# A mixture-of-experts block on one core: the router stage's work in a new order on all engines

## The chip, the cores and the metric

One core of a Trainium2 chip. The metric is the device time of one execution in microseconds (us). "Before" is the median of three runs of the kernel as it was.

## The reference

One layer of a decoder trunk over 1024 tokens of width 1024, all in float32. The parts that matter here come after the three mixers have left their outputs side by side in one row of 1024 per token (`ymix`):

```python
y   = ymix @ w_out                              # output projection
x2  = x + gate * rmsnorm(y) * g_post            # residual
h   = rmsnorm(x2) * (1 + scale) + shift         # input of the MoE
scores = sigmoid(h @ w_router)                  # 64 experts
biased = scores + e_bias
# 8 groups of 8 experts; the 4 groups with the best sum of their top 2
# then the 8 best experts of those groups
top_w = scores[top] / sum(scores[top]) * 2.5
shared = (silu(h @ ws1) * (h @ ws3)) @ ws2      # shared expert, width 256
# each expert e: its tokens through silu(xb @ w1[e]) * (xb @ w3[e]) @ w2[e]
```

## The kernel before, in words

The kernel runs in stages that follow each other: input projection and modulation, attention, the RWKV recurrence, the router stage (`norm_route`, L1530 to L2087), the 64 experts (`experts`, L2090) and the last norm. A stage is a block: every engine has its own written-out list of instructions, each in order, and semaphores join them. A new block starts when all engines have ended the old one.

The router stage works on 8 tiles (NT) of 128 tokens. Two lanes of buffers take turns: tile t uses lane t % 2. A lane has four banks of PSUM: t0 and t1 for transposes, for the router's product (t1) and the list positions (t0), p0 and p1 for the output projection, the shared expert's hidden layer (p1), its transposes (p0) and its result (p0, p1). Per tile the pieces are these, by the names that the code and the change use:

- TensorE (PE): `transpose_y` (L1957, 8 transposes), `project` (L1968, 48 matmuls: two halves n of 512 columns, 8 steps k, three passes of float32r parts), `up` (L1997, the shared expert's first layer, two halves of 12 matmuls), `transpose_h` (L2011, 8), `place` (L2020 and L2021, two small products that count the tokens before each one), `route` (L2027, the router's product in plain float32: 8 steps, 16 records of 64 columns), `transpose_act` (L2034, 2), `down` (L2042, 4 products in float32, 8 records of 512 columns).
- ScalarE (ACT): `y_norm` (L1688 to L1692: the squares of both halves, then the root), `y_cast` (L1682, L1683: high part of the next but one transposed tile), `x_norm` (L1697 to L1699), `h_copy` (L1706, L1707: transposed h out of PSUM, which `route` and `place` wait for), `h_cast` (L1711), `shared_sig` (L1716 to L1718), `score_exp` (L1723), `shared_out` (L1733), and once per kernel the four casts of the shared weights (L1756).
- VectorE (DVE): `x_rows` (L1780 to L1790: sum of squares, two scalings out of p0 and p1, and the addition of x), `y_rest` (L1770, L1771: low part of the transposed tile), `h_scaled` (L1798), `h_rows` (L1802), `shared_arg` (L1807), `shared_act` (L1814, L1815), `copy_act` (L1822), `logits` (L1827), `select` (L1832 to L1861, 26 small steps one after the other), `h_rest` (L1775), `places` (L1868 to L1872), and after the last tile `block_counts`, `block_ends`, `block_rows` (L1876 to L1896) and `first_rows` (L1900 to L1902).
- GpSimd (POOL): for each tile, after `places`, one store of the weights (L1657) and eight indirect scatters of token numbers into the experts' lists (L1659); after the last tile a gather of the list rows (L1663), which waits for all scatters, and four gathers of the first blocks' tokens (L1670).
- SyncE (SP): loads and stores, among them those of the shared result (L1642) and the loads of the first two experts' weights (L2365, L2372), in an order of its own, which waits for the same semaphores.

The order is written out in a loop over r from -1 to 9. In turn r, PE does `project(r+1)`, `transpose_y(r+2)`, `up(r-2)`, `transpose_h(r)`, `place(r-1)`, `route(r)`, `transpose_act(r-2)`, `down(r-2)`. DVE does `x_rows(r+1)`, `y_rest(r+2)`, `h_scaled(r+1)`, `shared_arg(r-2)`, `h_rows(r+1)`, `places(r-1)`, `shared_act(r-2)`, `logits(r)`, `copy_act(r-2)`, `select(r)`, `h_rest(r)`. The few waits that matter: `route(r)` waits for `h_copy(r)`; `transpose_act` for `shared_act`; `down` for `copy_act`; `transpose_h(r)` for `y_rest(r+2)`, since both use t0 and t1 of a lane; `project(t)` for `shared_out(t-4)`; `up(t)` for the scalings of tile t+2.

## Time and profile before

| | us |
|---|---|
| median of 3 runs | 1972.87 |
| lowest and highest run | 1970.88, 1981.24 |
| the profiled execution, its own time | 1981.13 |
| its span, first to last instruction | 1979.3 |
| router stage in it | 689.3 to 961.7 |
| PE busy over the span | 1770.1 (89%) |
| DVE, ACT, POOL busy | 1411.6, 1133.6, 454.5 |

The times of the trace are microseconds from the span's start. A matmul's end is modelled, so that the records of matmuls in a row overlap: what one costs is the distance between two starts. PEclk is the share of full speed that TensorE's clock was granted, 1.00 for 2.4 GHz and 0.50 for 1.2 GHz.

### The profile page before, as it was taken

How to read it: one execution, taken by the hardware profiler on the slowest of the kernel's cores; microseconds unless marked ns; L12 is line 12 of the kernel's file. 1: busy time of each engine (PE TensorE's matmuls, PEld its weight loads, DVE VectorE, ACT ScalarE, POOL GpSimd, SP SyncE). 2: the span in 40 equal slices, each digit the busy share in tenths (PEclk: the TensorE clock that was granted, in tenths of full speed). 3: DMA queues.
4: the chain of work that ended last, by engine and by line, in shares of the span. 5: the costliest groups of instructions: out<-in, count | busy, mean ns of one | idle time of the engine just before them, and what ended most of it. 6: DMA issues, size and time to landing. Idle time of an engine off the chain costs nothing. (4 is left out here: it accounts for less than half of the span.)

```text
span 1979.3 us, 38771 instructions
## 1 busy us (share of the span) xinstructions
PE 1770.1 (89%) x10357; PEld 1361.8 (69%) x10358; DVE 1411.6 (71%) x2637; ACT 1133.6 (57%) x2184; POOL 454.5 (23%) x361
## 2 busy tenths in 40 slices
PE   3899999777699788998599999999999999999992
PEld 3787887454488666765377777777777677777771
DVE  6587740687488566445388888888888788888885
ACT  3411220576466443322377777777777677777774
POOL 0011000000122103135122332333233333333331
PEclk9999999898799888988799999999999999999996
DMA  9267610300200163314779979799989989899965
GB/s 348 81 193 214 183 49 27 128 18 16 89 6 11 50 236 95 81 53 109 243 236 303 292 217 301 222 314 319 279 259 295 311 283 288 249 315 309 297 180 181
DMA packets 168094, 380.06 MB, mean 192 GB/s; under 512 B 31189, under 2 KB 43822, under 8 KB 164924
## 3 DMA queue, kind: packets, MB, share of 16 engines
q1 hardware_dynamic: 132844, 288.38, 41.9%
q0 software_dynamic: 35168, 90.60, 18.9%
q8 instruction: 50, 0.82, 0.2%
q14 instruction: 32, 0.26, 0.1%
HBM read 333.82 MB, written 82.13 MB: 210 GB/s over the span
## 5 line engine op out<-in xcount | busy, mean ns | idle before, releaser
L2267 DVE TENSOR_TENSOR w_low<-w_experts,w_high 128x1024 fp32r<-128x1024 f32 x392 | 462.0, 1220 | 103.6 <-issue 68.0
L2216 ACT CAST w_high<-w_experts 128x1024 fp32r x394 | 394.0, 1050 | 97.0 <-issue 77.2
L2198 POOL DMA_INDIRECT acc<-y_rows,scatter_idx x96 | 185.4, 1931 | 612.7 <-DMA acc<-y_rows,scatter_idx 354.2
L2329 PE MATMUL ps_h<-w_high,xT_high 128*128 128x512 f32 x776 | 315.9, 407 | 10.7 <-DVE xT_low L2282 10.5
L2329 PE MATMUL ps_h<-w_high,xT_low 128*128 128x512 f32 x776 | 307.7, 397 | 0.0
L2329 PE MATMUL ps_h<-w_low,xT_high 128*128 128x512 f32 x776 | 307.5, 396 | 0.0
L2351 PE MATMUL ps_y<-w_experts,actT 128*128 x384 | 182.1, 597 | 2.3 <-DVE actT_low L2273 2.3
L2329 PEld LDWEIGHTS ps_h<-w_high,xT_high 128*128 128x128 f32 x776 | 147.3, 190 | 43.4 <-issue 6.7
L2329 PEld LDWEIGHTS ps_h<-w_high,xT_low 128*128 128x128 f32 x776 | 146.2, 188 | 35.4
L2329 PEld LDWEIGHTS ps_h<-w_low,xT_high 128*128 128x128 f32 x776 | 146.6, 189 | 31.0
L2182 POOL DMA_INDIRECT gathered<-h,idx x96 | 130.5, 1359 | 58.1 <-DVE idx L2260 29.1
L2224 ACT CAST w_high<-w_experts 128x512 fp32r x192 | 110.2, 625 | 27.3 <-issue 24.4
L2276 DVE TENSOR_TENSOR w_low<-w_experts,w_high 128x512 fp32r<-128x512 f32 x192 | 123.2, 682 | 0.2
L2321 PEld LDWEIGHTS ps_x<-ident,gathered 128*128 128x128 f32 x784 | 103.9, 193 | 16.7 <-issue 7.7
L2355 PE MATMUL ps_y<-w_high,actT_high 128*128 128x512 f32 x192 | 114.5, 596 | 0.0
L2321 PE MATMUL ps_x<-ident,gathered 128*128 128x128 f32 x784 | 104.8, 277 | 6.9 <-PEq L1532 6.9
L506 PE MATMUL pbank<-w_in_high,hT_high 128*128 128x512 f32 x256 | 103.4, 404 | 6.8 <-DVE w_in_low L339 6.8
L506 PE MATMUL pbank<-w_in_low,hT_high 128*128 128x512 f32 x256 | 101.7, 397 | 0.0
L506 PE MATMUL pbank<-w_in_high,hT_low 128*128 128x512 f32 x256 | 101.4, 396 | 0.0
L2351 PEld LDWEIGHTS ps_y<-w_experts,actT 128*128 128x128 f32 x384 | 66.1, 192 | 48.7 <-issue 48.7
L884 POOL TENSOR_TENSOR r_k<-p_mixed,k 128x256 f32<-128x256 f32 x8 | 6.0, 748 | 341.1 <-DVE operands L1142 341.1
L2209 ACT CAST xT_high<-ps_x 128x512 fp32r<-128x512 f32 x98 | 57.4, 585 | 41.5 <-PE ps_x L2321 40.6
(440 smaller groups left out, 3627.6 us busy)
## 6 DMA issues: line engine op xcount, KB each, us to landing
w_experts<-in_exp_w SPq DMA_DIRECT2D x512, 256.0 KB
w_experts<-in_exp_w SPq DMA_DIRECT2D x128, 512.0 KB
qT<-in_w_ada POOLq DMA_DIRECT2D x16, 1024.0 KB, 7.8
w_raw<-in_w_in SPq DMA_DIRECT2D x24, 512.0 KB, 7.9
w_ada<-in_w_ada SPq DMA_DIRECT2D x8, 1024.0 KB, 12.0
p_mixed<-mixed SPq DMA_DIRECT2D x8, 512.0 KB, 8.3
w_out<-in_w_out SPq DMA_DIRECT2D x1, 4096.0 KB, 12.6
x_kept<-x SPq DMA_DIRECT2D x8, 512.0 KB
```

Source lines behind the costliest of these rows:

```text
L506: q = mm(bank[u % RING][:], lhs, rhs, start=(k == 0 and i == 0), stop=(k == KC - 1 and i == 2))
L2182: pool.indirect_dma_start(xg[j][:], None, dr["h2"], bass.IndirectOffsetOnAxis(ap=idx[j][:], axis=0), bounds_check=S - 1, oob_is_err=False) ...
L2198: pool.indirect_dma_start(dr["acc"], bass.IndirectOffsetOnAxis(ap=sidx[j][:], axis=0), y[j % 2][:], None, bounds_check=S - 1, oob_is_err=F ...
L2209: act.copy(xT[0][:, 0:4, :], ps_x[0][:].rearrange("p (k n) -> p k n", k=4))
L2216: act.copy(w13_s[par][0][:, which, k], w13[:, bass.ds(w, 1), which, k].squeeze(1)).then_inc(w_high, 1)
L2224: act.copy(w2_s[half][0], w2[:, bass.ds(w, 1), 1, half * BANK:(half + 1) * BANK].squeeze(1)).then_inc(d_high, 1)
L2267: dve.tensor_tensor(w13_s[par][1][:, which, k], w13[:, bass.ds(w, 1), which, k].squeeze(1), w13_s[par][0][:, which, k], ALU.subtract).then ...
L2276: dve.tensor_tensor(w2_s[half][1], w2[:, bass.ds(w, 1), 1, half * BANK:(half + 1) * BANK].squeeze(1), w2_s[half][0], ALU.subtract).then_in ...
L2321: q = pe.transpose(ps_x[k // 4][:, (k % 4) * P:(k % 4 + 1) * P], xg[j][:, 0:D].rearrange("p (c k) -> p k c", k=KC)[:, k, :], ident[:])
L2329: q = pe.matmul(ps_h[:].rearrange("p (a n) -> p a n", a=2), xT[a][:, k, :], w13_s[par][z][:, :, k, :], start=(k == 0 and m == 0), stop=(k ...
L2351: pe.matmul(ps_y[n][:], aT[:], w2[:, bass.ds(w, 1), 0, n * BANK:(n + 1) * BANK].squeeze(1), start=True, stop=False)
L2355: q = pe.matmul(ps_y[n][:], aT_s[a][:], w2_s[n][z], start=False, stop=(m == 2))
```

## The change

The lists of PE, ACT and DVE are put into a new order; no product, copy or sum is added or left out. SP's and POOL's lists stay as they are.

- PE, turn r from 0 to 6: `up(r-2)`, `place(r-2)`, `project(r+1)`, `transpose_act(r-2)`, `transpose_y(r+2)`, `down(r-2)`, `transpose_h(r)`. `route(r-1)` is no longer a piece of its own: two of its 8 steps follow each of the first four steps k of `project(r+1)`'s first half.
- A new semaphore, half_mm, comes after the projection's first half; ACT takes the squares of that half while the second half runs.
- `x_rows` is split: the addition of x is now `x_sum`, after `y_rest`.
- ACT and DVE follow: `h_copy`, `h_cast`, `score_exp`, `logits`, `h_rest` and `select` of tile r-1, and `places(r-2)`, now stand in turn r.
- What is left of the last three tiles after turn 6 is written out for each engine. PE waits for the list rows (rows_in) after all `down` pieces; before, `transpose_act(7)` and `down(7)` stood behind that wait.

```diff
             def y_norm(t):
                 w = lane[t % 2]
+                act.wait_ge(half_mm, t + 1)
+                act.activation(w.sq[:, 0:BANK], w.p0[:], ACT.Square, accum_out=w.st[:, 0:1])
                 act.wait_ge(proj_mm, t + 1)
-                act.activation(w.sq[:, 0:BANK], w.p0[:], ACT.Square, accum_out=w.st[:, 0:1])
                 act.activation(w.sq[:, BANK:], w.p1[:], ACT.Square, accum_out=w.st[:, 1:2]).then_inc(sq_done, 1)
                 act.wait_ge(ss_done, t + 1)
                 step.then(act.activation(w.st[:, 3:4], w.st[:, 2:3], ACT.Ln, scale=1.0 / D, bias=eps))
@@ -1736,26 +1737,36 @@
             for k in range(KC):
                 act.copy(w_out_s[0][:, k, :], w_out[:, k, :]).then_inc(wo_high, 1)
             y_cast(1)
...
+            for r in range(-1, NT - 1):
+                if r >= 1:
+                    h_copy(r - 1)
+                    h_cast(r - 1)
                 if r >= 2:
                     shared_sig(r - 2)
-                if 0 <= r < NT:
-                    score_exp(r)
-                    h_cast(r)
+                if r >= 1:
+                    score_exp(r - 1)
+                y_norm(r + 1)
+                if 0 <= r < NT - 2:
+                    y_cast(r + 2)
+                if r >= 2:
+                    shared_out(r - 2)
+                x_norm(r + 1)
                 if r == 0:
                     act.wait_ge(weights_in, 16 * 4)
                     for which, k in PIECES:
                         act.copy(ws13_s[0][:, which, k], ws13[:, which, k]).then_inc(ws_high, 1)
-                if r >= 2:
-                    shared_out(r - 2)
+            h_copy(NT - 2)
+            h_cast(NT - 2)
+            score_exp(NT - 2)
+            shared_sig(NT - 3)
+            h_copy(NT - 1)
+            h_cast(NT - 1)
+            shared_out(NT - 3)
+            score_exp(NT - 1)
+            shared_sig(NT - 2)
+            shared_sig(NT - 1)
+            shared_out(NT - 2)
+            shared_out(NT - 1)
...
                     dve.wait_ge(x2_out[t % 2], nth(t))
                 stt(w.x2[:, 0:BANK], w.p0[:], w.st[:, 4:5], post[:, 0:BANK], ALU.mult, ALU.mult)
                 stt(w.x2[:, BANK:], w.p1[:], w.st[:, 4:5], post[:, BANK:], ALU.mult, ALU.mult).then_inc(xn_done, 1)
+
+            def x_sum(t):
+                w = lane[t % 2]
                 dve.wait_ge(xn_done, t + 1)
                 dve.wait_ge(x_in[t % 2], nth(t) + 16)
                 tt(w.x2[:], w.x2[:], w.x[:], ALU.add).then_inc(x2_done, 1)
...
+            for r in range(-1, NT - 1):
+                if r >= 0:
+                    h_scaled(r)
+                    h_rows(r)
                 if r >= 2:
                     shared_arg(r - 2)
+                    places(r - 2)
                     shared_act(r - 2)
+                if r >= 1:
+                    logits(r - 1)
+                    h_rest(r - 1)
+                    select(r - 1)
                 if r >= 2:
                     copy_act(r - 2)
+                x_rows(r + 1)
+                if 0 <= r < NT - 2:
+                    y_rest(r + 2)
+                x_sum(r + 1)
                 if r == 0:
...
+            h_scaled(NT - 1)
+            h_rows(NT - 1)
+            places(NT - 3)
+            logits(NT - 2)
+            h_rest(NT - 2)
+            shared_arg(NT - 3)
+            shared_act(NT - 3)
+            copy_act(NT - 3)
+            select(NT - 2)
+            logits(NT - 1)
+            h_rest(NT - 1)
+            places(NT - 2)
+            select(NT - 1)
+            shared_arg(NT - 2)
+            shared_arg(NT - 1)
+            places(NT - 1)
+            shared_act(NT - 2)
+            block_counts()
+            copy_act(NT - 2)
+            block_ends()
+            block_rows()
+            shared_act(NT - 1)
+            copy_act(NT - 1)
+            first_rows()
...
-                if t == 0:
+                for k in range(KC if t == 0 else 0):
+                    pe.wait_ge(wo_low, k + 1)
+                    q = step(0, k)
+                    if k == KC - 1:
+                        q.then_inc(half_mm, 1)
+                    q = step(1, k)
+                for n in range(2 if t else 0):
+                    if t >= 4:
+                        pe.wait_ge(ysh_done, 2 * (t - 4) + n + 1)
                     for k in range(KC):
-                        pe.wait_ge(wo_low, k + 1)
-                        for n in range(2):
-                            q = step(n, k)
-                else:
-                    for n in range(2):
-                        if t >= 4:
-                            pe.wait_ge(ysh_done, 2 * (t - 4) + n + 1)
-                        for k in range(KC):
-                            q = step(n, k)
+                        q = step(n, k)
+                        if n == 0 and k < KC // 2 and t >= 2:
+                            route(t - 2, range(2 * k, 2 * k + 2))
+                    if n == 0:
+                        q.then_inc(half_mm, 1)
                 q.then_inc(proj_mm, 1)
...
-            def route(t):
+            def route(t, steps):
                 w = lane[t % 2]
-                pe.wait_ge(h2T_done, t + 1)
-                for k in range(KC):
+                if steps[0] == 0:
+                    pe.wait_ge(h2T_done, t + 1)
+                for k in steps:
                     q = mm(w.t1[:, 0:E], w.h2T[:, k, :], w_r[:, k, :], start=(k == 0), stop=(k == KC - 1))
-                q.then_inc(route_mm, 1)
+                if steps[-1] == KC - 1:
+                    q.then_inc(route_mm, 1)
...
+            for r in range(NT - 1):
+                if r >= 2:
+                    up(r - 2, 0)
+                    up(r - 2, 1)
+                    place(r - 2)
+                if r == 1:
                     pe.wait_ge(consts_in, 16 * 14)
                     pe.wait_ge(weights_in, 16 * 4)
+                project(r + 1)
+                if r >= 2:
+                    transpose_act(r - 2)
                 if r + 2 < NT:
                     transpose_y(r + 2)
...
                 if r >= 2:
                     down(r - 2)
+                transpose_h(r)
+
+            up(NT - 3, 0)
+            place(NT - 3)
+            route(NT - 2, range(KC))
+            up(NT - 3, 1)
+            transpose_h(NT - 1)
+            transpose_act(NT - 3)
+            down(NT - 3)
+            route(NT - 1, range(KC))
+            up(NT - 2, 0)
+            place(NT - 2)
+            up(NT - 2, 1)
+            up(NT - 1, 0)
+            up(NT - 1, 1)
+            place(NT - 1)
+            pe.wait_ge(pos_done, NT)
+            mm(ps_a[0:E, 0:1], seen[:], ones[:, 0:1], start=True, stop=True).then_inc(sched_mm, 1)
+            transpose_act(NT - 2)
+            pe.wait_ge(sched_sums, 1)
+            mm(ps_b[0:E, 0:1], upper[0:E, 0:E], nblk[:], start=True, stop=True).then_inc(sched_mm, 1)
+            pe.wait_ge(sched_ends, 1)
+            mm(ps_b[:, E:2 * E], nbc[:], upper[0:E, 0:E], start=True, stop=True)
+            mm(ps_a[:, 0:NB], ones[0:E, :], ind[:], start=True, stop=True)
+            mm(ps_b[:, 2 * E:2 * E + 1], ind[:, 0:P], ones[0:E, 0:1], start=True, stop=True)
+            mm(ps_b[:, 2 * E + 1:2 * E + 2], ind[:, 0:P], nblk[:], start=True, stop=True)
+            mm(ps_a[:, NB:2 * NB], slot_step[:], ind[:], start=True, stop=True).then_inc(sched_mm, 1)
+            down(NT - 2)
+            transpose_act(NT - 1)
+            down(NT - 1)
+            pe.wait_ge(rows_in, 16)
+            pe.transpose(ps_c[:, 0:P], list_rows[:], ident[:]).then_inc(rows_T, 1)
```

## Rows read from the trace of the kernel before

**Rows 1.** Busy time by stretch: turns 2 to 6, end, experts (first row: columns).
```profile
core 0: us, PE busy (x) PEld busy (x) DVE busy (x) ACT busy (x) POOL busy (x), PEclk, DMA share, GB/s
...
758.10:907.70 149.60, 137.95 (x584) 101.26 (x584) 83.52 (x274) 45.00 (x104) 47.80 (x51) 0.89 0.24 69
907.70:961.70 54.00, 40.02 (x151) 24.97 (x149) 18.33 (x75) 10.28 (x20) 25.71 (x26) 0.91 0.65 171
...
975.90:1979.30 1003.40, 957.92 (x4256) 731.64 (x4256) 812.64 (x1368) 756.51 (x1193) 315.87 (x192) 0.98 0.87 273
```

**Rows 2.** Busy time within turn 3 (tile 4 projected): three stretches, columns as rows 1.
```profile
800.30:808.90 8.60, 7.91 (x45) 6.62 (x43) 5.85 (x9) 5.42 (x15) 0.00 (x0) 1.00 0.54 172
808.90:812.90 4.00, 2.60 (x18) 2.07 (x18) 3.27 (x11) 2.22 (x6) 1.29 (x2) 0.88 0.43 165
812.90:819.50 6.60, 6.54 (x9) 2.83 (x10) 5.84 (x32) 0.83 (x2) 5.08 (x6) 0.55 0.02 1
```

**Rows 3.** Timeline of PE: project(1), turn 3, turn 7; start, length, piece, idle before.
```profile
707.78 0.39 PE L1968 MATMUL rbank<-w_out_high,h2T_high 128*128 128x512 f32 x1
...
806.78 1.03 PE L2011 MATMUL rbank<-ident,ymix_tile 128*128 128x128 f32 x8
...
808.98 2.00 PE L2027 MATMUL rbank<-router_w,h2T 128*128 128x64 f32 x16 [0.77 <-ACT h2T L1707]
...
919.06 3.70 PE L2042 MATMUL rbank<-shared_w,sh_actT 128*128 128x512 f32 x8 [0.52 <-DVE sh_actT L1822]
```

**Rows 4.** Timeline of PE, turns 0 and 1.
```profile
718.88 1.04 PE L1957 MATMUL rbank<-ident,h_tile 128*128 128x128 f32 x8
725.15 1.94 PE L2011 MATMUL rbank<-ident,h_tile 128*128 128x128 f32 x8 [5.23 <-DVE ymixT_low L1771]
...
731.69 0.77 PE L1968 MATMUL rbank<-w_out_high,ymixT_high 128*128 128x512 f32 x1
...
745.28 1.04 PE L1957 MATMUL rbank<-ident,y_shared 128*128 128x128 f32 x8
```

**Rows 5.** ACT: timeline at 733, groups of turn 3.
```profile
733.32 3.88 ACT L1756 CAST shared_w_high<-shared_w 128x1024 fp32r<-128x1024 f32 x4
...
L1697 ACT ACTIVATE squares<-x_tile 128x1024 f32<-128x1024 f32 x1 | 1.1, 1062 | 1.8 <-DVE x_tile L1790 1.8
...
L1688 ACT ACTIVATE squares<-rbank 128x512 f32<-128x512 f32 x1 | 0.6, 597 | 10.5 <-PE rbank L1968 10.5
...
L1706 ACT COPY h2T<-rbank 128x512 f32<-128x512 f32 x1 | 0.6, 586 | 0.9 <-PE rbank L2011 0.9
```

**Rows 6.** Timeline of DVE, turn 3.
```profile
802.56 0.75 DVE L1786 SCALAR_TENSOR_TENSOR x_tile<-rbank,norm_stats,post_scale 128x512 f32<-128x512 f32 x1 [0.60 <-ACT norm_stats L1692]
...
804.00 1.23 DVE L1790 TENSOR_TENSOR x_tile<-x_tile,x_in 128x1024 f32<-128x1024 f32 x1
...
812.82 0.35 DVE L1832 TENSOR_SCALAR scores<-scores 128x64 f32<-128x64 f32 x1
...
818.93 0.26 DVE L1861 TENSOR_SCALAR weights<-route_w,weight_sum 128x64 f32<-128x64 f32 x1
```

**Rows 7.** Timeline of POOL, the last two tiles and the gathers.
```profile
916.67 0.57 POOL L1657 DMA_DIRECT2D h<-weights  x1 [5.40 <-DVE list_dest L1872]
...
928.53 0.57 POOL L1657 DMA_DIRECT2D h<-weights  x1
...
947.10 0.98 POOL L1663 DMA_INDIRECT list_rows<-lists,list_row  x1 [7.80 <-DMA lists<-ids,list_dest]
954.02 1.04 POOL L1670 DMA_INDIRECT gathered<-h,idx  x1 [5.94 <-DVE idx L1902]
```

**Rows 8.** Timelines of PE and SP, the end of the stage.
```profile
952.12 0.48 PE L2080 MATMUL rbank<-ident,list_rows 128*128 128x128 f32 x1 [4.93 <-DMA list_rows<-lists,list_row]
...
961.36 0.33 SPq L1642 DMA_DIRECT2D acc<-x_tile  x1
...
967.57 1.97 PE L2321 MATMUL ps_x<-ident,gathered 128*128 128x128 f32 x8 [6.85 <-PEq L1532]
```

72 lines of the change are left out of this document (2 added, 70 removed).

## Prediction

> **What bounds the kernel now.** I read the busy time by stretch first, then the timelines of the engines inside the router stage. The reader should see that the experts' stage is 1003.4 of the span's 1979.3 us with PE nearly always busy, and that the change touches nothing in it [rows 1]. The router stage is bound by PE too, but not by its work. Turns 2 to 6 take 149.6 us, 29.9 each, with PE busy 137.95 and a granted clock of 0.89. Within one turn the clock is 1.00 until `place` is done, then 0.88 over 4 us in which PE waits 0.77 for the copy of h, runs `route`, waits for the shared expert's activation and for its copy; then it is 0.55, and `down` runs at 1.2 GHz: 6.6 us [rows 2, 3]. At full clock the same piece takes 3.70, as in turn 7 [rows 3]. So a turn pays some 2.2 us of waits and 2 to 3 us for the low clock. After turn 6 come 54.0 us with little PE work, bound by chains between engines [rows 1].
>
> The profiled execution took 1981.13 us, its span 1979.3; the median of the three runs is 1972.87, 8.3 lower. The sum is made against the profiled times, and the saving is taken off the median.
>
> **A turn in the new order, on PE.** At full clock: `project` is 48 matmuls in 718.88 - 707.78 = 11.1 us, 0.231 each [rows 3, 4], so `up`, 24 of the same, is 5.6. Eight transposes are recorded with 1.03, of which 0.17 overlaps the next piece: 0.85 for each of the two groups [rows 3]. `place`, four records like `route`'s 0.12: 0.5. `transpose_act` 0.3. `down` 3.5 (3.70 less the overlap). The router's product takes 2.00 us for 16 records of 64 columns, 1.9 without the overlap; they are bound by weight loads [rows 3].
> **Its bounds laid between steps.** No row shows these records amid the projection. If the loads hide wholly, the columns cost 16 x 64/512 x 0.231 = 0.5 us; if every load stands bare and the steps behind restart, I allow 3.0. I take 1.9, the nearest row.
> The Trainium skill, "TensorE: Matmul & The Clock Gate", Part 3, speaks against the interleaving: a load overlaps a running matmul only where the row groups differ. By that rule the product would cost nearer 3 us and the gain would be 6 us smaller. The trace disagrees for this kernel: in 8.6 us, loads are busy 6.62 and matmuls 7.91, so they overlap [rows 2].
> The turn is 5.6 + 0.5 + 11.1 + 1.9 + 0.3 + 0.85 + 3.5 + 0.85 = 24.6, and 0.1 for semaphores: **24.7 against 29.9**, 26.1 saved over five turns.
>
> **What must hide for that.** Let a turn's PE begin at 0; `up` and `place` end at 6.1, the projection at P = 19.1, the turn at 24.7.
> (a) *Copy of h(r-1) before the product.* From the last projection's end, P' = -5.6: half the squares 0.8, sum and root 0.8, two scalings 1.5, `y_rest` 1.3 and `x_sum` 1.2 give 5.6; `x_norm` 1.7 and the two copies 1.2 (0.59 each) [rows 5, 6] give P' + 8.5 = 2.9. `shared_out(r-3)` stands before `x_norm` on ACT but ends at P' + 5.2. PE asks at 6.8: 3.9 us spare.
> (b) *DVE.* The product ends at 10.7. `logits` 0.2, `h_rest` 1.2 and `select` (812.82 to 819.19, 6.4) [rows 6] end at 18.6; `copy_act` is asked for at 19.4. It is 0.43 long, under `transpose_y`'s 0.85. Spare 0.8. `h_scaled`, `h_rows`, `shared_arg`, `places`, `shared_act` (5.0 us in all) lie before 8.6.
> (c) *`transpose_h(r)` waits for `y_rest(r+2)`*, which ends at P + 4.4: squares' first half goes under the projection (0.6) and x's addition behind (1.23), so 1.8 sooner than now. PE arrives at P + 4.65. Spare 0.2, so the first of the three to fail.
> (d) *Queues.* `places` stands earlier on DVE, and POOL's nine issues, 928.53 - 916.67 = 11.9 us at most [rows 7], fit in 24.7. SP's list is not moved: the store of acc(r-2) now stands behind the wait for h(r+1), about 10 us after P, with `load_y` behind it; both are asked for over a turn later. `shared_out` two tiles on waits for that store, 49 us later. Cost nothing; without this cover, `project` would wait for `shared_out`.
>
> **The start.** `transpose_h(0)` ran at 725.15 for 1.94, released by `y_rest(2)` [rows 4]; by (c) it comes 1.8 sooner and ends at 725.2. `project(2)` does its first step, then waits for h(0)'s copy, which ACT now does after `x_norm(1)` and the four casts of the shared weights, 3.88 us [rows 5]: 726.1 + 3.9 + 1.1 = 731.1. From there 45 matmuls 10.4, product 1.9, and the low clock after the wait, 13.6 - 11.1 = 2.5 as in the old `project(2)` [rows 4]: 745.9. `transpose_h(1)` has the same chain ahead of it as `transpose_h(0)`, 6.3 us from group to group [rows 4]; less 1.8 it starts at 750.4 and ends, at low clock, 1.9 later: 752.3. The old turn 2 began at 758.1, with `place(0)` and `route(1)` done as well; the new turns do those, and leave `place(5)` and `route(6)`, so the contents are equal. New start 752.3, 2.0 for the restart at low clock, five turns 123.5: **877.8 against 907.7**.
>
> **The end.** From 877.8 = 0: half `up(5)`, `place`, `route(6)`, half `up`, 8.0; `shared_arg`, `shared_sig`, `shared_act` 2.9 (PE idle about 2); transposes and copy 1.1; `down(5)` 3.5, `route(7)` 1.9, half `up(6)`, `place(6)` give 20.7, and `places(6)` 22.0. From here POOL holds the chain: scatters of tiles 6 and 7, 11.3 us each, 44.6. `places(7)`, due at 31, and `block_rows` at 36 are earlier. Then 2.0 for the last scatter to land, 5.0 for the gather of list rows (947.10 to 952.12), 1.9 to the first token gather, four of them 4.9 [rows 7, 8]: 58.4. I add 0.6 for a slower clock somewhere: **936.8**. Before, the stage ended at 961.7 with the store of acc(7) [rows 8], as `transpose_act(7)` waited behind the list rows; that wait leaves the path. The last landing is the loosest price: from 1 us to the 7.8 that POOL was idle before 947.10 [rows 7]; the row gather could take longer beside the second expert's weights, whose load SP issues some 7 us before it instead of with it: I allow 5 more.
> The new block's first transposes come 5.9 us after the stage's end, as before [rows 8]; the experts' loads and gathers follow their own semaphores and just move with it.
> **Sum:** 961.7 - 936.8 = 24.9. Profiled 1981.1 - 24.9 = 1956.2; median 1972.9 - 24.9 = **1948.0**.
>
> **The rivals.**
> 1. *DVE becomes the bound.* If `select` or `y_rest` ends some 2 us later than I laid out, (b) and (c) fail and each turn takes 2 us more: 1958. For it: the spares of 0.8 and 0.2. Against: DVE is busy only 83.5 of 149.6 us. Chance 0.10.
> 2. *The product's loads hide,* about 1 us for each of six tiles: 1942. Chance 0.08.
> 3. *`down` stays at the low clock.* It would now follow two groups of transposes, as the old one followed transposes and small products. Five times 2.9 (6.6 - 3.7) and about 3 in the end: 1948.0 + 17.5 = 1965.5. Against: the old stretch ahead of it was 6 us long, the new one 1.2 [rows 2, 3]. Turn 7 had 5 us of it and kept full clock. Chance 0.07. The Trainium skill, same page, Part 4, says that transposes do not count as busy PE; by that rule this rival would be the case to fear, and the trace neither shows nor excludes it.
> 4. *Slower: PE halts inside `project`.* The copy of h(r-1) stands on ACT behind `shared_out(r-2)` and `x_norm(r)`. If it comes later than the 3.9 us spare, PE stops amid the first half, every us costs one, and about 2 us of low clock follow. It decides from halts of 3 us in each of five turns (3 + 2 = 5.0 a turn, the whole gain); at 4 us: 1948 + 30 = 1978. For it: such a halt of 5 us is in my sum at the start. Against: every step of (a) has a row. Chance 0.03.
>
> **Numbers.** The forecast has 0.72. A measurement of this kernel can tell 0.5% (9.9 us) from no change: the bound is 1963. The forecast, rivals 1 and 2 and a sliver of 3 are faster, 0.91; most of rival 3 is within, 0.06; rival 4 is slower, 0.03. Range: the product's price gives -8 to +7 (1.4 less or 1.1 more, six times), landings -1 to +11, the start's clock 1; not all together. With rivals 1 and 2 inside, 1939 to 1960; rivals 3 and 4 are left out.
>
> **What would show it.** Starts of `up` 24.7 us apart; clock 1.00 in `down`, 3.5 us; one halt of 5 us in `project(2)` and none in later ones; `transpose_h` without idle time before it; POOL without a pause from `places(6)` on; stage ending near 937; experts at 1003 us as before. It is wrong if turns take over 27 us, if ACT's copy releases PE in each, or if the stage's gain does not arrive at the end.

## The result, and the profile after

The changed kernel took **1961.81 us** (median of 15 runs, 1953.41 to 1973.4); the kernel before, on the same chips, 1978.09 (15 runs, 1970.88 to 1987.03). The ratio is 0.9915, with a 95% interval of 0.9895 to 0.9934: 16.3 us faster by the medians, 13 to 21 by the interval. The forecast of 1948.0 is 13.8 too low, and the range ended at 1960. Two things add up: the median shown before, of three runs, was 5.2 lower than that of fifteen, and 24.9 us of saving were forecast where 16.3 came (8.6). The range of 1939 to 1960, taken off the 1972.87 of three runs, is a saving of 12.9 to 33.9; the 16.3 lie inside it. With the base of fifteen runs the range would have been 1944 to 1965.

The profiled execution took 1954.59 us, its span 1952.8, which is 26.5 below the one of before. 6.2 of that lie ahead of the router stage, where nothing was changed: the stage's first transposes start at 683.10 here and 689.29 there. One profile of each kernel is therefore not enough to read the saving from; the experiments took more of both.

Busy time by stretch, columns as in [rows 1] (the router stage's start, its five even turns, its end, the step to the experts, the experts):
```profile
683.10:745.50 62.40, 49.17 (x209) 40.61 (x209) 39.40 (x70) 28.25 (x52) 0.00 (x0) 0.80 0.60 209
745.50:867.80 122.30, 121.73 (x585) 95.29 (x583) 78.73 (x243) 44.81 (x104) 45.81 (x45) 0.99 0.32 89
867.80:932.80 65.00, 41.96 (x172) 28.52 (x169) 27.11 (x112) 13.48 (x27) 30.05 (x32) 0.86 0.57 158
932.80:948.90 16.10, 1.97 (x8) 1.58 (x9) 5.95 (x8) 7.15 (x9) 0.00 (x0) 0.50 0.55 187
948.90:1952.80 1003.90, 959.51 (x4256) 733.06 (x4256) 813.37 (x1368) 756.80 (x1193) 318.50 (x192) 0.98 0.87 273
```
Five turns in 122.3 us with PE busy 121.73 and the clock at 0.99: PE has nothing left to wait for. Against [rows 1] the turns are as forecast or better; the end is not, 65.0 us where the forecast has 59.0, and the step to the experts is longer too.

The timeline of PE (start, length, piece; in brackets the idle time before and what ended it): the halt in `project(2)`, the second group of transposes of h, and in a late turn `down` with its neighbours.
```profile
724.62 1.11 PE L2058 MATMUL rbank<-router_w,h2T 128*128 128x64 f32 x4 [4.30 <-ACT h2T L1708]
...
743.85 1.94 PE L2041 MATMUL rbank<-ident,ymix_tile 128*128 128x128 f32 x8 [3.46 <-DVE ymixT_low L1782]
...
838.16 0.38 PE L2066 MATMUL rbank<-ident,sh_act 128*128 128x128 f32 x2
838.38 1.04 PE L1983 MATMUL rbank<-ident,y_shared 128*128 128x128 f32 x8
839.25 3.60 PE L2074 MATMUL rbank<-shared_w,sh_actT 128*128 128x512 f32 x8
842.68 1.04 PE L2041 MATMUL rbank<-ident,ymix_tile 128*128 128x128 f32 x8
```
No bracket stands at `down` or at the transposes behind it, and `down` takes 3.60 where turn 3 of before had 6.6 [rows 2].

The end, on POOL, SP and PE, to be read against [rows 7, 8]:
```profile
912.19 0.97 POOL L1659 DMA_INDIRECT lists<-ids,list_dest  x1 [0.30 <-issue]
919.26 0.98 POOL L1663 DMA_INDIRECT list_rows<-lists,list_row  x1 [6.10 <-DMA lists<-ids,list_dest]
927.85 1.04 POOL L1670 DMA_INDIRECT gathered<-h,idx  x1 [7.61 <-DVE idx L1916]
...
931.79 0.99 POOL L1670 DMA_INDIRECT gathered<-h,idx  x1 [0.30 <-issue]
...
916.00 0.33 SPq L1642 DMA_DIRECT2D acc<-y_shared  x1
916.37 4.80 SPq L2404 DMA_DIRECT2D w_experts<-in_exp_w  x8
...
925.96 0.48 PE L2126 MATMUL rbank<-ident,list_rows 128*128 128x128 f32 x1 [6.34 <-DMA list_rows<-lists,list_row]
940.63 0.69 PE L2360 MATMUL ps_x<-ident,gathered 128*128 128x128 f32 x2 [14.20 <-PEq L1532]
```
The last scatter is issued by 913.16. It lands 6.1 us later (forecast 2.0); the rows' gather takes 6.7 to PE's transpose (5.0); 7.85 us lie between the last token gather and the experts' first transposes.

### The profile page after: what moved, and what is told of

It reads as the page before. It is cut to its first block and busy times, and to the rows that moved or that the text cites. A ratio compares the mean times of both kernels' runs of the same rounds, so it can differ in the third digit from the quotient of the medians.

```text
span 1952.8 us, 38762 instructions
## 1 busy us (share of the span) xinstructions
PE 1748.2 (90%) x10357; PEld 1352.4 (69%) x10358; DVE 1412.6 (72%) x2637; ACT 1135.2 (58%) x2184; POOL 458.8 (23%) x361
## 5 line engine op out<-in xcount | busy, mean ns | idle before, releaser
L2368 PE MATMUL ps_h<-w_high,xT_high 128*128 128x512 f32 x776 | 316.9, 408 | 10.6 <-DVE xT_low L2321 10.1
L2221 POOL DMA_INDIRECT gathered<-h,idx x96 | 131.4, 1369 | 58.5 <-DVE idx L2299 29.9
## 6 DMA issues: line engine op xcount, KB each, us to landing
w_out<-in_w_out SPq DMA_DIRECT2D x1, 4096.0 KB, 12.4
```

Source lines behind the costliest of these rows:

```text
L2221: pool.indirect_dma_start(xg[j][:], None, dr["h2"], bass.IndirectOffsetOnAxis(ap=idx[j][:], axis=0), bounds_check=S - 1, oob_is_err=False) ...
L2368: q = pe.matmul(ps_h[:].rearrange("p (a n) -> p a n", a=2), xT[a][:, k, :], w13_s[par][z][:, :, k, :], start=(k == 0 and m == 0), stop=(k ...
```

## The experiments

Below, *landing* is the idle time of POOL between the last list scatter and the gather of the rows. What varies ahead of the stage and behind it is kept out of the comparison by measuring from the stage's first transposes: to the end of the last scatter's issue, and to the experts' first transposes.

**The turn: interleaving or order?** The router's product as one piece again:
```
@@ project
-                        if n == 0 and k < KC // 2 and t >= 2:
-                            route(t - 2, range(2 * k, 2 * k + 2))
@@ loop of the tensor engine
+                if r >= 1:
+                    route(r - 1, range(KC))
                 project(r + 1)
```


> The changed kernel with the router's product of a tile again one piece of 8 products ahead of the output projection, not two by two behind its first four steps. Theory (the gain is the order of the turn, and the product costs the tensor engine about its own 1.8 us wherever it stands): the turn stays at 24.35 us or grows by at most 0.2 us, the router stage stays within 1 us of 249.7 us. Rival A (the product laid between the steps is what saves: as one piece its small matmuls cost what they cost in the kernel before, some 3 us): the turn grows by 1 us or more, the stage by 5 us or more. Rival B (as one piece it comes before the projection's first step and halts the engine on the copy of h, which is ready 3.9 us ahead of the first product now): a gap opens ahead of the product in every turn, growing the turn by what the copy is late.

Ratio to the kernel before 0.9945 (0.9924 to 0.9966). Starts of `up` at 781.40, 805.76, 830.11, 854.47: the turn is 24.36 us, as with the interleaving, and the product's row reads 1.95 us. The gain is the order's; sixteen records, four behind each of four steps, cost the same 1.8 together. At the start the halt stands before the first step of `project(2)` rather than behind it (5.68 us, ended by the copy of h), and the turns begin 1.7 us later. Rivals A and B fall. What was expected of the whole stage did not hold: to the last token gather it took 256.8 us, not 249.7, since here the last scatter took 12.89 us to land, not 6.10. The saving in total is 11.8 us by the medians, 4.5 less than with the product interleaved; the intervals overlap, and beyond the 1.7 us at the start no row says whether that is real.

**The spare of 0.2 us.** The early squares, and `y_rest` ahead of `x_sum`, undone:
```
@@ y_norm
-                act.wait_ge(half_mm, t + 1)
-                act.activation(w.sq[:, 0:BANK], w.p0[:], ACT.Square, accum_out=w.st[:, 0:1])
                 act.wait_ge(proj_mm, t + 1)
+                act.activation(w.sq[:, 0:BANK], w.p0[:], ACT.Square, accum_out=w.st[:, 0:1])
@@ loop of the vector engine
+                x_sum(r + 1)
                 if 0 <= r < NT - 2:
                     y_rest(r + 2)
-                x_sum(r + 1)
```


> The changed kernel without its early squares: both halves of a tile's squares wait for the whole projection, and the vector engine takes the sum of the x columns ahead of the rest of y again. Theory (the turn is the tensor engine's own work with little to spare ahead of the transposes of h, 0.2 us by the prediction): the rest of y and h come 1.5 to 2 us later, the tensor engine halts 1 to 2 us ahead of the transposes of h in each turn, the turn grows from 24.35 to 25.4 to 26.2 us, the stage by 5 to 10 us. Rival (the spare was underrated and the small moves of the scalar and vector engines do nothing; the order on the tensor engine alone carries the gain): turn 24.35 to 24.6 us, no gap, stage within 1.5 us of 249.7 us.

Ratio 0.9964 (0.9941 to 0.9987). The timeline of PE, in two turns:
```profile
803.90 1.06 PE L2040 MATMUL rbank<-ident,ymix_tile 128*128 128x128 f32 x8 [1.58 <-DVE ymixT_low L1781]
...
830.02 1.06 PE L2040 MATMUL rbank<-ident,h_tile 128*128 128x128 f32 x8 [1.58 <-DVE ymixT_low L1781]
```
The idle time reads 1.58 us, but the record of `down` ahead of it covers some of the loss: from the start of `down` to that of the transposes it is 5.18 us, where the changed kernel has 3.43, so the halt costs 1.75. The rest of y came 1.84 us later (6.13 us behind `transpose_act`'s start, not 4.29), so the spare of step (c) was about 0.1 us, half of the 0.2 forecast. The turn is 26.13, and stage start to experts' transposes is 272.4 us against 257.5 to 263.9. Two lines on ACT and DVE carry 1.8 of the 5.5 us that a turn gained on [rows 1].

**The end alone, on the old turns.**
```
@@ last turn of the old order, tensor engine (vector engine likewise)
-                if r == NT + 1:
-                    pe.wait_ge(rows_in, 16)
-                    pe.transpose(ps_c[:, 0:P], list_rows[:], ident[:]).then_inc(rows_T, 1)
                 if r >= 2:
                     transpose_act(r - 2)
...
                 if r >= 2:
                     down(r - 2)
+                if r == NT + 1:
+                    pe.wait_ge(rows_in, 16)
+                    pe.transpose(ps_c[:, 0:P], list_rows[:], ident[:]).then_inc(rows_T, 1)
```


> The kernel before with one thing of its last turn moved: the transposes and the down product of tile 7 and the vector engine's copy for it stand ahead of the wait for the list's rows, not behind it. This is the new end's order alone, on the old turns. Theory (the end is the chain GpSimd scatter, gather of the rows, transpose, token gathers, and the down product was behind it only in SyncE's and PE's queues): stage 272.4 us becomes 269 to 271 us. Rival (the end of the stage is set by the scatters' chain alone, and the down product hides in any place): stage within 0.7 us of 272.4 us. In both the turns stay at 29.9 us.

Ratio 1.0017 (0.9993 to 1.0041): nothing gained, and a stage of 269 to 271 us did not come. Here the scatter landed in 11.98 us where the first profile of the old kernel had 7.80, so a small gain of the `down` product could be hidden in the trace behind that. The forecast's "that wait leaves the path" was worth no measurable time.

**What holds the landing?** First the load of expert 1's weights, moved ahead in SyncE's list:
```
-                if r == NT + 1:
+                if r == NT:
                     sp.wait_ge(up_mm, NT)
                     load_up(sp, io, keep, 1, 1)
                     load_down(sp, io, keep, 1, 1)
```


> The changed kernel with the load of expert 1's weights issued one step earlier in SyncE's program: as soon as the last up product is done (about 898 us on the trace's clock), not behind the store of tile 6's output at 916 us. Theory A (this load, set off by the late down product, fills the queues under the gather of the list's rows and the token gathers): the list-rows gather takes 5.0 us again, not 6.7, and the step to the experts' first transposes 6 us, not 7.85; the last scatter may land sooner or later. Stage shorter by 1.5 to 2.5 us, the whole by 2 to 5 us. Theory B (the scatter's landing of 6.1 us, the gather's 6.7 us and the handover's 7.85 us are latencies that spread from run to run or come of themselves): all three within 1 us of those, stage within 1 us of 249.7 us. Rival C (the load now falls on the scatters themselves, 891 to 913 us): scatters land later, stage longer by 1 to 4 us.

Ratio 0.9917 (0.9892 to 0.9943). Landing 15.81, the longest of all; then the gather of the rows, 2.98. The queues were busy with the load through the whole landing. In this profile that fits part of A and part of C, that the load delays whatever small transfer it runs beside; the stage was not shorter (263.2 us to the experts' transposes). Three more kernels on one chip followed: the unedited one, one with the store and the load held back to the landing of the rows, and one with the load alone held back.
```
@@ both held (in the other kernel this wait stands before load_up of expert 1)
                     sp.wait_ge(ysh_done, 2 * t + 2)
+                    if t == NT - 2:
+                        sp.wait_ge(rows_in, 16)
                     sp.dma_start(dr["acc"][rows(t), :], lane[t % 2].ysh[:]).then_inc(acc_out[t % 2], 16)
```


> The changed kernel itself, unedited, beside the three below on one chip. It tells how far one kernel's end spreads: in the changed kernel's profile the last list scatter was followed by 6.1 us before the gather of the list's rows, in the kernel before by 7.8 us, in the three edited changed kernels and the edited old one so far by 12.9, 14.2, 15.8 and 12.0 us. Theory A (a 512 KB store of a tile's output, or the weights' load behind it, that SyncE issues within some 2 us of the last scatter or under it holds the scatter's landing; later ones do not): here, where the store again comes 2 to 3 us behind the last scatter, 6 to 8 us; where it comes sooner, 12 to 16 us. Theory B (it is the chip or the execution): 6 to 16 us with no relation to the store's place. Turns 24.35 us either way; total 1955 to 1972 us.

> The changed kernel with one wait more on SyncE: the store of tile 6's output, and with it the load of expert 1's weights and the store of tile 7's output behind it, wait for the gather of the list's rows. Nothing big moves while the last scatters land and the list's rows are gathered. Theory A (the store and the load hold the landing): the last scatter lands in 2 to 4 us (6.1 in the changed kernel's profile), the rows' gather takes 4 to 5 us to the transpose (6.7), so the stage is 5 to 7 us shorter than 249.7 us, 10 to 14 us shorter than where the landing took 13 to 16 us. Theory B (landing is the scatters' own latency): 6 us or more with an idle queue, stage within 1 us. Rival C (the 4.2 MB then fall on the four token gathers and on what the next block fetches): the first transposes of the experts come 8 us or more behind the last gather, and the gain is given back there.

> As the last, but only the load of expert 1's weights (and tile 7's store behind it) waits for the rows' gather; the store of tile 6's output keeps its place 2 to 3 us behind the last scatter. If the 512 KB store is what holds the scatter's landing: landing as in the unedited kernel of this job, gather of the rows 5 us. If the weights' load is: landing 2 to 4 us, as with both held.

Ratios 0.9914 (0.9886 to 0.9942), 0.9897 (0.9867 to 0.9927) and 0.9928 (0.9901 to 0.9956): no two can be told apart by their time. The unedited kernel's end:
```profile
928.62 0.99 POOL L1663 DMA_INDIRECT list_rows<-lists,list_row  x1 [13.62 <-DMA lists<-ids,list_dest]
...
912.08 7.67 SPq L2404 DMA_DIRECT2D w_experts<-in_exp_w  x8
...
949.08 1.97 PE L2360 MATMUL ps_x<-ident,gathered 128*128 128x128 f32 x8 [14.29 <-PEq L1532]
```
The load began 2.9 us before the scatter's issue was over, and the landing took 13.62, as theory A has it. With both held:
```profile
914.49 0.97 POOL L1661 DMA_INDIRECT lists<-ids,list_dest  x1 [0.30 <-issue]
924.28 0.98 POOL L1665 DMA_INDIRECT list_rows<-lists,list_row  x1 [8.82 <-DMA lists<-ids,list_dest]
...
927.39 0.47 PE L2128 MATMUL rbank<-ident,list_rows 128*128 128x128 f32 x1 [11.42 <-DMA list_rows<-lists,list_row]
945.91 0.48 PE L2362 MATMUL ps_x<-ident,gathered 128*128 128x128 f32 x1 [18.05 <-PEq L1532]
```
The landing still takes 8.82 us, not 2 to 4, with nothing else in the queues. The queue view of the same kernel, from 917.5 to 924.2 us (from two microseconds behind the last issue to the gather's):
```profile
DMA packets 0, 0.00 MB, mean 0 GB/s; under 512 B 0, under 2 KB 0, under 8 KB 0
```
All packets of the scatters had gone by 917.5, and for 6.7 us more no semaphore came. With the load alone held it was 8.55: no sign that the 512 KB store matters, from one profile of each. The gather of the rows fell to 3.11 and 2.80 us. But the last gather was followed by 11.7 and 13.0 us before the experts' transposes, not 7.9: the held load now ran beside the next block's start, as rival C had it, and took the gain back there. That the load is the reason there is inferred from these two and the next kernel; no wait in the trace names it.

**Three repairs at once.** (1) The copy of h(0) ahead of the casts, which go to the next turn; (2) a new order of the last three tiles; (3) store and load held.
```
@@ (1) scalar engine
+                if r == 1:
+                    act.wait_ge(weights_in, 16 * 4)
+                    for which, k in PIECES[:2]:
+                        act.copy(ws13_s[0][:, which, k], ws13[:, which, k]).then_inc(ws_high, 1)
                 if r >= 1:
                     score_exp(r - 1)
@@ (2) tensor engine (cut here and below: a few more pieces move)
                 route(NT - 2, range(KC))
-            up(NT - 3, 1)
             transpose_h(NT - 1)
-            transpose_act(NT - 3)
-            down(NT - 3)
+            up(NT - 3, 1)
             route(NT - 1, range(KC))
             up(NT - 2, 0)
             place(NT - 2)
+            transpose_act(NT - 3)
             up(NT - 2, 1)
+            down(NT - 3)
@@ (2) vector engine
+            select(NT - 2)
             shared_arg(NT - 3)
-            shared_act(NT - 3)
-            copy_act(NT - 3)
-            select(NT - 2)
```


> Three repairs of the changed kernel at once. First, the copy of h(0) ahead of the shared weights' casts on the scalar engine, with the vector engine's subtractions moved to the next turn, so that the output projection of tile 2 no longer halts 4.3 us behind its first four steps. Second, the end's order: select(6) right behind the rest of h(6), the transposes of h(7) ahead of the second half of up(5), the product of tile 7 ahead of up(6), so that GpSimd's scatters of tiles 5, 6 and 7 run without a pause (now 7.4 us stand between tiles 5 and 6). Third, the store of tile 6's output and the load of expert 1 behind the gather of the list's rows. Theory: 4 to 6 us from the first, 4 to 7 us from the second (the vector engine's copies for down(5) come later, which may give back 1 to 2), 5 to 7 us from the third: stage 233 to 238 us against 249.7, total 12 to 18 us under the changed kernel of this job. Rival: the first only moves the halt (the casts then hold score and squares of the next turn, and the engine stops there instead), 0 us; the second and the third overlap, since a landing that is not held needs no earlier scatter: total 5 to 9 us under.

Ratio 0.9890 (0.9863 to 0.9918), 1.5 us under the unedited kernel of its job by the medians. (1) works: the halt of 4.30 is 0.53, and turns start 2.7 us earlier. (2) gave 0.6 us only; the reason stands on DVE:
```profile
898.76 0.23 DVE L1893 TENSOR_TENSOR left<-rbank,list_at 128x64 f32<-128x64 f32 x1 [5.73 <-DMA lists<-ids,list_dest]
```
The places of tile 7 wait for the landing of tile 5's scatters, whose buffer they reuse; these were issued by 882.9 and landed 15.9 us later, beside expert 0's weights. With (3) the landing took 5.65. The gather of the rows reads 4.50, but SyncE, which waits for it too, went on 3.0 us behind its issue: PE came late, since the new order had `down(7)` still running. The step to the next block took 12.4, and the experts' part 1020.2 us, 9 more than in the unedited kernel's profiles (1010.9 on the mean); why, no row here tells. Against the unedited kernel of its job the way to the experts is 8.2 us shorter (255.7, 263.9), the total 1.5, of 12 to 18 expected.

**The load in the next block, and a version of everything.** `e11` takes expert 1's load out of the stage; `e12` has (1), (2), a buffer of its own for tile 7's places, and that load.
```
@@ router stage, SyncE
-                if r == NT + 1:
-                    sp.wait_ge(up_mm, NT)
-                    load_up(sp, io, keep, 1, 1)
-                    load_down(sp, io, keep, 1, 1)
@@ experts, SyncE, both places
-                if after is not None or s >= PREFETCHED:
+                if after is not None or s >= 1:
@@ e12 only
+        dest_of = lambda t: dest7 if t == NT - 1 else lane[t % 2].dest
...
-                if t >= 2:
+                if 2 <= t < NT - 1:
                     dve.wait_ge(lists_out[t % 2], nth(t) * TOP_K)
```


> The kernel before, unedited, one more profile, to tell how its own end spreads. In its first profile SyncE issued the store of tile 6's output 1.4 us behind the last list scatter and the load of expert 1's weights 7.9 us behind it, just when the scatter had landed (7.8 us). Theory A (the weights' load holds the landing, and the old order issues it too late to do so): landing 6 to 9 us again. Theory B (the landing spreads by itself between 6 and 16 us in every kernel): anywhere in that range. The edited old kernel had 12.0 us with the load coming 7.9 us behind, which speaks a little for B.

> The changed kernel with the load of expert 1's weights taken out of the router stage and issued by SyncE at the start of the experts' block, where expert 1 is some 50 us or more from being needed. Theory A (that load, now issued beside the last list scatters, holds their landing, and where it is held back to the token gathers it holds the next block's first instructions instead: 11.7 to 13 us from the last gather to the experts' first transposes, against 7.9 us): landing 6 to 9 us as with the load held, and 7.5 to 8 us from the last gather to the first transposes; from the stage's start to the experts' first transposes 254 to 257 us, against 263.9 us of the unedited kernel in the last job, 257.5 us in its first profile. Theory B (the handover's 11.7 to 13 us were its own spread): no relation. Rival C (experts start to wait for expert 1's weights or for those of expert 2 behind them): the experts' part grows over 1012 to 1017 us by what is late.

> The changed kernel with: the copy of h(0) ahead of the shared weights' casts (worth 2.8 us in the last job's run of all three repairs); the end's new order, now with a buffer of its own for tile 7's list places, so that they no longer wait for the landing of tile 5's last scatter (15.9 us behind its issue, which gave back what the order had won); and expert 1's load in the next block. Theory: 2.8 us, 3 to 5 us from the scatters without pause, 6 to 9 us from the landing, handover 7.5 to 8 us: from the stage's start to the experts' first transposes 246 to 250 us, whole kernel 12 to 16 us under the changed one. Rival: the landing of tile 7's last scatter waits for all earlier ones in the queue, so that issuing them earlier moves nothing (landing longer by what the issue is earlier): 253 us or more.

> The changed kernel unedited on the same chip as the three above, to compare with. Where SyncE issues the load of expert 1 under the last scatter: landing 12 to 16 us, from the stage's start to the experts' first transposes 263 us or so; where it issues it 3 us behind, 6 us and 257 us. Total 1955 to 1970 us.

Ratios 0.9899 (0.9873 to 0.9926) for e11, **0.9865** (0.9838 to 0.9892) for e12, 0.9920 (0.9899 to 0.9941) for the changed kernel beside them: medians of 1961.25, 1952.99 and 1964.98 us. Only e12 stands clear of the changed kernel. In e11 the landing takes 9.92, the gather 2.78, the step to the experts 7.79 (257.4 us from the stage's start), and the experts' part is no longer (1012.7). In e12 the last scatter's issue ends 222.8 us behind the stage's start (229.7 in the kernel beside it), but lands 11.05 later; 252.0 us to the experts, 2 more than the 246 to 250 expected, because of that landing. Part of the rival holds: the issue ended 7.3 us earlier than in e11, the landing 6.2. The further profiles of both plain kernels showed how loose one sample is:
```profile
927.25 0.98 POOL L1663 DMA_INDIRECT list_rows<-lists,list_row  x1 [10.70 <-DMA lists<-ids,list_dest]
...
919.72 5.64 SPq L2404 DMA_DIRECT2D w_experts<-in_exp_w  x8
...
940.48 0.98 POOL L1663 DMA_INDIRECT list_rows<-lists,list_row  x1 [13.54 <-DMA lists<-ids,list_dest]
...
936.03 3.94 SPq L2365 DMA_DIRECT2D w_experts<-in_exp_w  x8
```
The first two lines are the changed kernel beside e11 and e12. Its load comes 3.2 us behind the last scatter's issue, as in the first profile, and its landing takes 10.70 us, not 6.10. The last two are the *old* kernel, the load coming 9.1 us behind: 13.54, not 7.80. So the load's place cannot be all of it, and theory A, by which the first would have been 6 us again, fails as a rule for one landing.

**Marks.** GpSimd waits for each landing and then clears a few words, which the timeline shows:
```
                 pool.dma_start(dr["h2"][rows(t), D:], w.wt[:]).then_inc(W_out[t % 2], 16)
+                if t in (1, 3):
+                    pool.wait_ge(W_out[t % 2], nth(t) + 16)
+                    pool.memset(mark[:, 3 * t:3 * t + 1], 0.0)
                 for n in range(TOP_K):
...
+                    if n == 0 and t in (2, 4):
+                        pool.wait_ge(lists_out[t % 2], nth(t) * TOP_K + 16)
+                        pool.memset(mark[:, 3 * t + 1:3 * t + 2], 0.0)
+                if t < NT - 1:
+                    pool.wait_ge(lists_out[t % 2], (nth(t) + 16) * TOP_K)
+                    pool.memset(mark[:, 3 * t + 2:3 * t + 3], 0.0)
```


> The changed kernel with expert 1's load in the next block, and marks on GpSimd, where it has time to spare between tiles: behind the eight list scatters of each tile but the last it waits for their landing and clears a few words, so that the profile shows each landing; in tiles 2 and 4 it does the same behind the first scatter alone, in tiles 1 and 3 behind the plain 32 KB store of the weights ahead of the scatters. Theory A (the landing is the delay of the completion of any such transfer on this queue, or of its own kind): one scatter alone takes as long from its issue to the mark as the last of eight, both 5 to 14 us, in all tiles. Theory B (eight scatters in a row of 128 words each pile up behind each other in memory): one alone 2 to 3 us, the last of eight 6 us or more. Rival C (other traffic in the queues sets it): short in tiles where nothing big is loaded, long where loads and stores of tiles run beside. The plain store: 2 to 4 us in all theories, if the scatter's way of writing is the cause; as long as a scatter, if it is the queue.

> The same marks in the changed kernel itself, for a second sample of each landing; at the end with expert 1's load beside the last scatters: 10 to 14 us there, the others as in the run before within 2 us if the landing depends on the place in the stage, at random if it spreads by itself.

> The kernel of all repairs once more, to see whether its time holds: ratio to the kernel before 0.984 to 0.989. From the stage's start to the experts' first transposes 246 to 254 us, less by 5 where the last scatter lands in 6 us in place of 11.

> A third profile of the kernel before: from the stage's start to the experts' first transposes 275 to 282 us as in the two others (277 and 278), with landing between 6 and 14 us; in each theory the average gain of the change there is near 16 us, not the 24.9 of the prediction.

> As the first kernel with marks, but in tiles 3, 4, 5 and 6 only four of the eight list scatters are issued (it leaves out half of those tiles' entries in the experts' lists, so the experts compute less). Theory B (scatters in a row pile up behind each other): the last of four lands in about half the time that the last of eight took in the same tiles (5.8, 6.7, 10.3 and 6.7 us in the first kernel with marks; 4.7, 6.6, 11.4 and 8.2 in the second), so 2.5 to 4.5 us in tiles 3, 4 and 6, the tiles with eight as before: 9.8 to 14 us in tiles 0 to 2. Theory C alone (the other traffic of the place sets it, and the number does not matter): 5 to 7 us in tiles 3, 4, 6 and 10 to 11 us in tile 5, beside the loads of weights.

The marks of the first kernel: L1664 behind eight scatters (tiles 0 to 6), L1661 behind one (tiles 2 and 4), L1656 behind the plain store (tiles 1 and 3). The bracket is the landing:
```profile
778.16 0.10 POOL L1664 MEMSET mark<- 128x1 f32 x1 [12.35 <-DMA lists<-ids,list_dest]
784.28 0.10 POOL L1656 MEMSET mark<- 128x1 f32 x1 [5.21 <-DMA h<-weights]
808.15 0.10 POOL L1664 MEMSET mark<- 128x1 f32 x1 [13.68 <-DMA lists<-ids,list_dest]
815.16 0.10 POOL L1661 MEMSET mark<- 128x1 f32 x1 [4.89 <-DMA lists<-ids,list_dest]
837.82 0.10 POOL L1664 MEMSET mark<- 128x1 f32 x1 [13.12 <-DMA lists<-ids,list_dest]
839.86 0.10 POOL L1656 MEMSET mark<- 128x1 f32 x1 [1.23 <-DMA h<-weights]
857.41 0.10 POOL L1664 MEMSET mark<- 128x1 f32 x1 [5.82 <-DMA lists<-ids,list_dest]
861.15 0.10 POOL L1661 MEMSET mark<- 128x1 f32 x1 [1.63 <-DMA lists<-ids,list_dest]
877.24 0.10 POOL L1664 MEMSET mark<- 128x1 f32 x1 [6.71 <-DMA lists<-ids,list_dest]
898.61 0.10 POOL L1664 MEMSET mark<- 128x1 f32 x1 [10.33 <-DMA lists<-ids,list_dest]
916.35 0.10 POOL L1664 MEMSET mark<- 128x1 f32 x1 [6.70 <-DMA lists<-ids,list_dest]
```
The landing of tile 7's eight, in front of the gather of the rows:
```profile
932.31 0.98 POOL L1668 DMA_INDIRECT list_rows<-lists,list_row  x1 [4.91 <-DMA lists<-ids,list_dest]
```
With four scatters in tiles 3 to 6 (the other four are left out, so the experts' lists are incomplete):
```profile
853.28 0.10 POOL L1666 MEMSET mark<- 128x1 f32 x1 [4.53 <-DMA lists<-ids,list_dest]
869.60 0.10 POOL L1666 MEMSET mark<- 128x1 f32 x1 [3.47 <-DMA lists<-ids,list_dest]
894.88 0.10 POOL L1666 MEMSET mark<- 128x1 f32 x1 [7.45 <-DMA lists<-ids,list_dest]
909.75 0.10 POOL L1666 MEMSET mark<- 128x1 f32 x1 [4.10 <-DMA lists<-ids,list_dest]
```

| landing, us, by tile | 0 | 1 | 2 | 3 | 4 | 5 | 6 | 7 |
|---|---|---|---|---|---|---|---|---|
| last of eight, first kernel | 12.35 | 13.68 | 13.12 | 5.82 | 6.71 | 10.33 | 6.70 | 4.91 |
| last of eight, second kernel | 10.95 | 10.79 | 9.78 | 4.74 | 6.63 | 11.37 | 8.23 | 9.89 |
| third kernel: last of eight (0 to 2, 7), of four (3 to 6) | 10.33 | 11.76 | 11.34 | 4.53 | 3.47 | 7.45 | 4.10 | 7.27 |
| one scatter, by kernel | | | 4.89, 5.77, 5.48 | | 1.63, 1.55 | | | |
| plain store, by kernel | | 5.21, 4.15, 3.99 | | 1.23, 1.65 | | | | |

Two things matter. *The number*: in tiles 4 to 6, four scatters land in 0.5 to 0.72 of the time of eight; in tile 3 they take 4.53, hardly less than eight in the second kernel (4.74; 5.82 in the first). Those places are not equally quiet, though: in tile 4 the DMA engines' share during the landing was 0.65 and 0.22 with eight and 0.01 with four. The cleaner comparison takes landings with a share of at most 0.02: 1.6 us for one (tile 4), 3.5 and 4.1 for four (tiles 4 and 6), 4.9 for eight issued after all earlier ones had landed (tile 7, first kernel), 8.8 for the last of sixteen in a row, in the kernel with both held. *The place*: tiles 0 to 2, where loads and stores of tiles run, and tile 5, beside expert 0's weights, take 9.8 to 13.7 us for eight, and in tile 2 one scatter alone takes 4.9 to 5.8. In tile 7 the second kernel, which has expert 1's load in the stage, took 9.89, the third, beside stores only, 7.27. So theory A of the first marks falls, and B and C hold together, B by the quiet landings; that the traffic is what makes a place slow is what the shares suggest, and no run moved only the traffic. Nor need it run during the landing: the one scatter of tile 2 in the third kernel was issued while the share was 0.46 to 0.66, no packet was left from 817.0 on, and it was released 4.7 us later. From the first to the second kernel a landing differs by 0.1 to 3.3 us. The totals of the three kernels with marks (single runs of 1966.68, 1969.04 and 1952.03 us) say nothing on speed, as the marks cost time and the last one does less work.

The repeated kernel of all repairs took 1952.15 us, ratio 0.9861 (0.9838 to 0.9883), with a landing of 13.43 and 252.6 us to the experts: its time holds. The third profile of the old kernel landed in 8.77 us.

## Why the prediction was wrong

All profiles of the two unedited kernels, from the start of the stage's first transposes, in us:

| | issue of the last scatter ends | landing | from that issue's end to the experts' first transposes | sum |
|---|---|---|---|---|
| before, three profiles | 250.0, 243.4, 246.3 | 7.80, 13.54, 8.77 | 28.3, 33.9, 29.5 | 278.3, 277.3, 275.8 |
| changed, three profiles | 230.1, 229.8, 229.7 | 6.10, 13.62, 10.70 | 27.5, 34.1, 32.9 | 257.5, 263.9, 262.5 |
| forecast | 233.1 | 2.0 | 20.3 | 253.4 |

The means of the sums are 277.1 and 261.3: 15.8 saved in the stage, beside a measured 16.3. The experts' part is the same to 1 us (means 1011.8 and 1010.9).

- **The turn** (24.7): right, 24.35. The old turn is the looser figure: in its other profiles `down` ran at full clock (3.70) in two and in one of the turns 2 to 6, and such turns take 27.2 us, not 29.9; in the profile shown none did. That is how these profiles reach the last scatter in 243.4 and 246.3 us. The product's 1.9 was 1.8; `down` kept the clock in all five turns, at 3.60 to 3.70. Of rival 3 nothing came: with two groups of transposes a turn the granted clock was 0.99 over the five turns. The rule behind it, that transposes do not count as busy PE (the Trainium skill, "TensorE: Matmul & The Clock Gate", Part 4), cost nothing here.
- **The spares**: (a) and (b) held; (c), 0.2 us, was about 0.1, as undoing it shows. No rival 1, no rival 4.
- **The start**: right. The halt was 4.3 (5 forecast), released by the copy of h behind the casts; taking the casts away, with the other two repairs, started the turns 2.7 us earlier.
- **Up to the last scatter** the forecast saves 16.9 us (250.0 to 233.1); the means save 16.7. That agreement is luck: the old profile shown was the slowest of three there, 3.4 above their mean of 246.6, and the forecast of the new was 3.3 above its mean of 229.8. The shown pair has 19.9: `down(5)` at the low clock (5.4, not 3.5) and `places(6)` at 23.5, not 22.0, were smaller losses than the turns' gain.
- **The failed step: "2.0 for the last scatter to land".** Bounded by 1 and 7.8, it was taken near the lower end, and 5.8 us of the saving rested on it alone. It measures 6.1 to 13.6 in the changed kernel and 7.8 to 13.5 in the old one: no gain at all (means 10.1 and 10.0). The nearest row was the 7.8 that [rows 7] shows for that same wait, and nothing in the change shortens it. That the old kernel's waits were due to something the new order removes was supposed, never read from a row. Of the 8.0 us of saving forecast beyond the last scatter's issue, the rest is the handover below, less the 0.6 added for the clock.
- **The rows' gather**, 5.0: on the mean 6.5 (6.7, 5.7, 7.1), where the old kernel has 5.0, 5.9 and 6.4; without the load in the queues 2.8 to 3.1. The bound named the load and the sum left it out. Step (d), "cost nothing", missed this place: SyncE's list was not moved, but what releases it was, and expert 1's load went from 7.7 to 9.1 us behind the last scatter to between 2.9 ahead and 3.2 behind.
- **The handover**: 5.9 was measured from the old stage's last store on SyncE; from GpSimd's last gather it was 8.6 already in the old profile, and 6.8 to 8.2 in all others that had not held the load back. In the new kernel GpSimd's gather is last, so the price of that engine counts: 7.9 to 8.2, 2 us more than forecast. The old kernel's other two profiles say the same: 3.7 and 4.5 us from that store, but 7.5 from the gather. So the wait of `down(7)`, which "leaves the path", seems not to have been what the step waited for.
- **The base**: three runs for the median, 5.2 us low. Without that the range would have held the time; the landing would have been as wrong.

With the forecast's own steps, and the waits behind the last scatter priced as they stood in the old rows (7.8, 5.0, 6.8 for the rest of the gathers, 8.6), the saving would have been the 16.9 to the last scatter alone: 1972.9 - 16.9 = 1956.0 from the median shown, and 1978.1 - 16.9 = 1961.2 from that of fifteen runs. That this is so near the 1961.81 owes something to the two errors of 3 us above, which cancel.

What stays open: why four profiles of the same place spread over 5.7 us (the old kernel's 7.80, 13.54, 8.77 and, edited, 11.98; likewise the changed kernel's 6.10, 13.62 and 10.70), and what it is in memory that makes scatters pile up. That three tiles in a row pile deeper than two was not isolated: 11.05 and 13.43 us for three tiles with pauses of at most 3.1 us between them, 8.55 to 9.92 for two with no weights' load beside them, yet 5.65 for three with pauses of 2.2 and 4.5.

## What to carry to other kernels

Price a wait that the change leaves alone at what its row shows, even where it looks like idle time that a shorter path ought to remove; where a row is a latency, take several profiles of it before anything rests on it. A transfer whose issue hangs on a semaphore moves with that semaphore: for each one, ask what small transfer on the path it will now run beside, and see whether a load that has time can go where none is waited for (here the rows' gather fell from between 5.7 and 7.1 us to between 2.8 and 3.1 in the traces; no total shows it by itself). And a block's end is paid by the engine that ends last, each at its own price.

## What the runs showed of the hardware

- The landing of a list scatter (128 words of 4 bytes) where the queues were quiet is 1.6 us, that of the last of four 3.5 and 4.1, of eight 4.9; after two tiles in a row, with queues that showed no packet for 6.7 us, 8.8, and after three 11.1. The Trainium skill, "DMA: Bandwidth & Descriptors", section on the anatomy of one DMA, gives a fixed cost of some 2 us, most of it the receipt of the write, and adds that HBM can make it surprisingly long. The 1.2 to 1.7 us of single transfers in quiet places are near it; for the last of a row of scatters it is 3.5 to 15.8 us here.
- A plain 32 KB store took 1.2 to 1.7 us to land in a quiet place and 4.0 to 5.2 beside other loads and stores. The same page of the Trainium skill, on queues, rings and completion order, says that a semaphore's increment lands only after every earlier write of that DMA engine, across its queues; the longer landings beside stores and piled scatters are what that would look like, but no run isolates it.
- From GpSimd's last gather to the next block's first matmul it took 6.8 to 8.6 us, and 11.7, 12.4 and 13.0 in the three kernels in which the load had been held back and ran beside the step.
- Sixteen records of small matmuls of 64 columns cost 1.8 us together, in one piece or four by four between steps of the projection: the turn is 24.36 and 24.35 us. Theirs is the one price that no row showed, and the old row of the whole piece gave it.
